# Attention's value products with the values on the left, the probabilities of two query heads moving, and the result turned back

## What is computed

```python
def sink_attention(q, k, v, mask, sink):
    s = jnp.einsum('bnqhgd,bnchd->bnhgqc', q, k).astype(jnp.float32) * (HEAD_DIM ** -0.5)
    s = jnp.where(mask[None, :, None, None], s, NEG_BIG)
    sink_col = jnp.broadcast_to(sink..., s.shape[:-1] + (1,))
    prob = jax.nn.softmax(jnp.concatenate([s, sink_col], axis=-1), axis=-1)[..., :-1]
    return jnp.einsum('bnhgqc,bnchd->bnqhgd', prob.astype(v.dtype), v)

def window_attention_prompt(q, k, v, sink):
    # blocks of WINDOW = 128 queries; each reads the 16 meta rows, the block before and itself
    keys = jnp.concatenate([meta(k), band(kb)], axis=2)
    vals = jnp.concatenate([meta(v), band(vb)], axis=2)
    ...

def merge(att_o, ga, hg_o, gh, hg_norm_w, w_out):
    att = att_o.reshape(*lead, ATT_WIDTH) * jax.nn.silu(ga)
    ...
```

## Time and profile before

| | before |
|---|---|
| median of 3 runs | 1170.9 us (1170.76 to 1171.3) |
| the profiled execution | 1167.6 us |
| its span | 1165.8 us |
| TensorE busy | 1129.7 us, 97% of the span |
| VectorE, ScalarE, GpSimd busy | 61%, 37%, 31% |
| mean granted clock of TensorE | 0.992 |

### The profile page before, as it was taken

One profiled execution on the slowest core, in us unless ns is written; L12 is line 12 of the kernel. 1 busy time (PEld: TensorE's weight loads), 2 busy tenths in 40 slices (PEclk: granted clock), 3 DMA queues, 4 the chain that ended last, 5 costly groups with the idle time before them and its releaser, 6 DMA issues.

```text
span 1165.8 us, 26052 instructions
## 1 busy us (share of the span) xinstructions
PE 1129.7 (97%) x9506; PEld 943.5 (81%) x9506; DVE 712.0 (61%) x1847; ACT 430.4 (37%) x1242; POOL 362.4 (31%) x420
## 2 busy tenths in 40 slices
PE   6999999999999999998879999999999999999998
PEld 5877888888888888887667888888888888688887
DVE  6657666666666666668745556555665666655443
ACT  6412212222222222215124555555565665433230
POOL 0003333333333333334422223222322227243331
PEclk9999999999999999999989999999999999999999
DMA  8532111111111111127022511211121133443431
GB/s 281 182 109 74 50 62 63 63 63 63 63 63 54 63 63 63 46 82 270 26 91 74 201 46 45 81 54 45 46 79 59 46 106 133 158 146 144 150 139 72
DMA packets 49391, 108.33 MB, mean 93 GB/s; under 512 B 5088, under 2 KB 17888, under 8 KB 49312
## 3 DMA queue, kind: packets, MB, share of 16 engines
q1 hardware_dynamic: 49328, 107.51, 25.9%
HBM read 70.23 MB, written 38.26 MB: 93 GB/s over the span
## 4 chain that ended last, share of the span: by engine, by line
PE 88%; DVE 5%; POOL 3%; issue 1%; ACT 1%; DMA 1%; SPq 1%; DVEq 0%; POOLq 0%; ACTq 0%
PE h_bank_b L917 5%; PE h_bank_a L917 5%; PE h_bank_b L919 5%; PE h_bank_b L918 5%; PE h_bank_a L919 5%; PE h_bank_a L918 5%; PE o_bank L2621 4%; PE o_bank L2623 4%; PE o_bank L2622 4%; PE h_bank_t L901 3%; PE a_bank_a L1891 3%; PE a_bank_a L1892 3%; PE a_bank_a L1893 3%; PE a_bank_b L1891 3%; PE a_bank_b L1892 3%; PE a_bank_b L1893 3%
## 5 line engine op out<-in xcount | busy, mean ns | idle before, releaser
L917 PE MATMUL h_bank_b<-h_w_hi,h_h_hi 128*128 128x512 f32 x256 | 106.5, 416 | 0.1
L1682 DVE CUSTOM_DVE_ANT_0 a_sm<-a_sc,a_hidden,a_neg_sink 128x272 f32<-128x272 f32 x128 | 59.0, 499 | 74.1 <-PE a_sc L1921 74.0
L917 PE MATMUL h_bank_a<-h_w_hi,h_h_hi 128*128 128x512 f32 x256 | 103.1, 403 | 0.0
L919 PE MATMUL h_bank_b<-h_w_hi,h_h_lo 128*128 128x512 f32 x256 | 100.9, 394 | 0.0
L918 PE MATMUL h_bank_b<-h_w_lo,h_h_hi 128*128 128x512 f32 x256 | 100.4, 392 | 0.0
L919 PE MATMUL h_bank_a<-h_w_hi,h_h_lo 128*128 128x512 f32 x256 | 99.9, 390 | 0.0
L918 PE MATMUL h_bank_a<-h_w_lo,h_h_hi 128*128 128x512 f32 x256 | 99.8, 390 | 0.0
L1488 ACT ACTIVATE a_prb<-a_sm,a_neg_m 128x256 f32<-128x256 f32 x128 | 64.2, 502 | 70.9 <-DVE a_neg_m L1682 70.8
L1891 PE MATMUL a_bank_a<-a_w_hi,a_h_hi 128*128 128x512 f32 (+1 forms) x208 | 77.0, 370 | 6.1 <-DMA a_h_lo<-h_split 6.1
L1892 PE MATMUL a_bank_a<-a_w_lo,a_h_hi 128*128 128x512 f32 (+1 forms) x208 | 74.1, 356 | 0.0
L1893 PE MATMUL a_bank_a<-a_w_hi,a_h_lo 128*128 128x512 f32 (+1 forms) x208 | 74.1, 356 | 0.0
(11 more groups left out here) (327 smaller groups left out, 3121.3 us busy)
## 6 DMA issues: line engine op xcount, KB each, us to landing
h_split<-h_h_hi SPq DMA_DIRECT2D x17, 512.0 KB, 3.0
h_split<-h_h_lo SPq DMA_DIRECT2D x17, 512.0 KB, 3.9
a_h_hi<-h_split SPq DMA_DIRECT2D x17, 512.0 KB, 3.4
a_h_lo<-h_split SPq DMA_DIRECT2D x17, 512.0 KB, 4.3
h_x<-x_prompt SPq DMA_DIRECT2D x16, 512.0 KB, 3.4
o_m<-mixed SPq DMA_DIRECT2D x16, 512.0 KB, 4.0
o_x<-x_prompt SPq DMA_DIRECT2D x16, 512.0 KB, 4.3
y_prompt<-o_x SPq DMA_DIRECT2D x16, 512.0 KB, 2.6
```

What stands on the lines that cost most here:

```text
L917: pe.matmul(out[:, :], h_hi[t.slot][:, k, :], hi, start=(k == 0), stop=False)
L919: ins = pe.matmul(out[:, :], h_lo[t.slot][:, k, :], hi, start=False, stop=(k == KT - 1))
L1682: ins = dve.tensor_tensor_reduce(SM[j % 2][:, i, :], sc[:, i, 0:KEYS], hidden[:, mask, :], -SCALE, neg_sink[:, h:h + 1], ALU.add, ALU.min, ...
```

## The change

The roles in the value products are exchanged: the 64 columns of a value head are the left operand, and the turned probabilities of two query heads of its group, 256 columns, are the moving one. The two value heads write the lower and the upper 64 partitions of `bank_o`, that is, stand at the left and the right half of the array. To make this possible a pair now holds one query head of each group (`head(j, i)`), PTS is twice as large and laid out by value head and block of keys, and there are two values steps for a tile, each for two pairs. VMD, the block-diagonal matrix of the meta values, is laid out in four blocks of 128 columns, and its product is four products with PMT moving. The result stands with the channels on the partitions; it is copied out by ScalarE (`copy_o`, to MIX), turned back by four transposes (`turn_o`) into `bank_o`, and normalized from there to MIX, which `mix` then multiplies in place (o_nat is gone).

The order changes with it. On VectorE `o_norm(last)` moves behind `maxima(t0, 0)`. On ScalarE `copy_o(last)` stands between `gate(t0)` and `place_q(t0, 1)`. On TensorE `turn_o(last)` stands behind `scores(t0, 0)`, and the query projection is split four and four instead of five and three. GpSimd's order stays. At the stage's end some pieces of the output stage's list are cut finer, so that `copy_o` and `turn_o` of the last tile fit between them.

```diff
+        PTS = sb("pts", [P, KVH, 2, 2, P])
...
+        def head(j, kv):
+            return kv * G_HEADS + j
...
-                sp.dma_start(VMD[h * META:(h + 1) * META, h * HD:(h + 1) * HD], V_meta[:, kv * HD:(kv + 1) * HD]).then_inc(v_meta_spread, 16)
+                kv, g = h // G_HEADS, h % G_HEADS
+                at = g * P + kv * HD
+                sp.dma_start(VMD[h * META:(h + 1) * META, at:at + HD], V_meta[:, kv * HD:(kv + 1) * HD]).then_inc(v_meta_spread, 16)
...
-                wait(pool, mix_stored, 16 * t.n)
-                pool.tensor_tensor(MIX[:, :], o_nat[:, :], G[t.slot][:, :], ALU.mult).then_inc(mix_done, 1)
+                pool.tensor_tensor(MIX[:, :], MIX[:, :], G[t.slot][:, :], ALU.mult).then_inc(mix_done, 1)
...
+            def copy_o(t):
+
+                act.wait_ge(o_ready, 2 * t.n - 1)
+                wait(act, mix_stored, 16 * t.n)
+                act.activation(MIX[:, :], bank_o[:, :], ACT.Copy).then_inc(o_copied, 1)
...
                 gate_plus(t0)
+                place_v(t0)
+                maxima(t0, 0, mask)
                 if tail:
                     o_norm(last)
-                place_v(t0)
-                maxima(t0, 0, mask)
...
-                for i in range(2):
-                    h = 2 * j + i
-                    kv = h // (AH // KVH)
-                    c, out = slice(kv * HD, (kv + 1) * HD), bank_o[:, h * HD:(h + 1) * HD]
-
-                    pe.matmul(out, PTS[:, i, 0:P], V[0][:, c], start=(h == 0), stop=False)
-                    ins = pe.matmul(out, PTS[:, i, P:2 * P], V[1][:, c], start=False, stop=False)
+                for block in range(2):
+                    for kv in range(KVH):
+                        c = slice(kv * HD, (kv + 1) * HD)
+                        ins = pe.matmul(bank_o[c, 2 * a * P:2 * (a + 1) * P], V[block][:, c],
+                                        PTS[:, kv, block, :, :].rearrange("p g q -> p (g q)"),
+                                        start=(a == 0 and block == 0), stop=False, skip_group_check=True)
                 ins.then_inc(pv_done, 1)
-                if j == 3:
-                    pe.matmul(bank_o[:, :], PMT[:, :], VMD[:, :], start=False, stop=True).then_inc(o_ready, 1)
+                if a == 1:
+                    for g in range(G_HEADS):
+                        c = slice(g * P, (g + 1) * P)
+                        ins = pe.matmul(bank_o[:, c], VMD[:, c], PMT[:, :], start=False, stop=True, skip_group_check=True)
+                    ins.then_inc(o_ready, 1)
+
+            def turn_o(t):
+
+                pe.wait_ge(o_copied, t.n)
+                for g in range(G_HEADS):
+                    c = slice(g * P, (g + 1) * P)
+                    ins = pe.transpose(bank_o[:, c], MIX[:, c], ident[:, :])
+                ins.then_inc(o_ready, 1)
```

More of the change, by code:

```diff
@@ L1542, in iteration @@
                 gate(t0)
+                if tail:
+                    copy_o(last)
                 place_q(t0, 1)
@@ L1580, in scalar @@
             gate(t0)
+            copy_o(tile(0, TILES - 3))
             place_q(t0, 1)
@@ L1610, in scalar @@
             place_p(end, 3)
+            yield
+            copy_o(end)
             yield
@@ L1709, in place_v @@
                 dve.wait_ge(v_copied, t.n + 1)
-                wait(dve, pv_done, 4 * (t.n - 1))
+                wait(dve, pv_done, 2 * (t.n - 1))
                 if first_tile(t):
@@ L1841, in vector @@
             gate_plus(t0)
-            o_norm(last)
             place_v(t0)
             maxima(t0, 0, t0.slot)
+            o_norm(last)
             k_stats(end)
@@ L2036, in tensor @@
             project(t2, kv_bank(t2), 2, range(4, 8)).then_inc(g_proj, 1)
-            values(t1, 2)
             turn_p(t1, 3)
+            pe.wait_ge(v_meta_spread, AH * 16)
             pe.wait_ge(k_placed, 3)
@@ L2047, in iteration @@
                 if tail:
-                    values(last, 3)
+                    values(last, 1)
                 pe.wait_ge(q_placed, 2 * t0.n - 1)
@@ L2054, in iteration @@
                 pe.wait_ge(g_copied, t0.n + 1)
-                project(t1, q_bank(t1), 1, range(0, 5))
+                if tail:
+                    turn_o(last)
+                project(t1, q_bank(t1), 1, range(0, 4))
                 turn_p(t0, 0)
                 scores(t0, 1)
-                project(t1, q_bank(t1), 1, range(5, 8)).then_inc(q_proj, 1)
-                values(t0, 0)
+                project(t1, q_bank(t1), 1, range(4, 8)).then_inc(q_proj, 1)
                 turn_p(t0, 1)
@@ L2064, in iteration @@
                 project(t1, kv_bank(t1), 2, range(0, 4))
-                values(t0, 1)
+                values(t0, 0)
                 turn_p(t0, 2)
@@ L2070, in iteration @@
                 project(t1, kv_bank(t1), 2, range(4, 8)).then_inc(g_proj, 1)
-                values(t0, 2)
                 turn_p(t0, 3)
@@ L2084, in tensor @@
             project(end, kv_bank(end), 0, range(0, 4))
-            values(tile(0, TILES - 3), 3)
+            values(tile(0, TILES - 3), 1)
             pe.wait_ge(q_placed, 2 * t0.n - 1)
@@ L2090, in tensor @@
             pe.wait_ge(g_copied, t0.n + 1)
+            turn_o(tile(0, TILES - 3))
             project(end, q_bank(end), 1, range(0, 4))
@@ L2114, in tensor @@
             yield
-            values(t0, 3)
+            values(t0, 1)
             pe.wait_ge(q_placed, 2 * end.n - 1)
@@ L2123, in tensor @@
             scores(end, 2)
-            values(end, 0)
             turn_p(end, 1)
@@ L2127, in tensor @@
             scores(end, 3)
-            values(end, 1)
+            values(end, 0)
             turn_p(end, 2)
             yield
-            values(end, 2)
             turn_p(end, 3)
             yield
-            values(end, 3)
+            values(end, 1)
+            yield
+            turn_o(end)
             yield
@@ L2826, in _ @@
             next(o)
+            next(a)
+            next(o)
         @block.vector
```

57 lines of the change are left out of this document (29 added, 28 removed).

## The result

The changed kernel takes **1194.1 us** (median of 5 runs, 1191.4 to 1196.1) against 1170.8 us before (median of 5, 1169.9 to 1171.3): ratio 1.0209, 95% interval 1.0195 to 1.0224. It is **23.4 us slower**. The forecast was 1191.3 us.

What follows compares the result with a forecast made beforehand. TensorE, busy 307.27 of 307.30 us, was taken to bound the attention stage, two feeders only just in time; +20.5 us for 13 iterations and -0.1 at the ends gave 20.4, so 1191.3 us, range 1175 to 1213.

Steps and rivals of the forecast that it cites:

- TensorE's own work: Values steps, meta product and turning back on TensorE: 3.88 us a tile instead of 4.23, a gain of 0.35 us.
- The two halves at once: In a values step, products at the array's left and right half run together: four rounds of 0.22, 1.28 us a step.
- the halves take turns: Rival: the array's halves run one after the other, values step 1.94 us or more, total 1212 to 1225; chance 0.10.
- Steps 1 to 6 of the chain: Pair 0's maxima, normalization, gate product, keys' power, keys' split, pair 1's exponentials; TensorE waits 1.3 us, turn 0.85 later.
- Step 4: Keys' power on GpSimd, 0.69 us: input ready at S+2.6, queues behind the product with the gate, ends S+4.31.
- The wait for the low halves: TensorE, before turning the next tile's queries, waits for their low halves from GpSimd: a new wait of 0.69 us.
- The iteration: One loop iteration of the attention stage, 13 alike (tiles 2 to 14): +1.58 us each, +20.5 us together.
- Tile 1: Tile 1's wait for pair 2's exponentials shrinks and the slow clock there goes: -1.9 us.
- Tile 15: Tile 15 has the two new waits but loses small ones at the hand-over: +0.8 us.
- The hand-over: Tile 16, into the output stage: copy, turning back and later gate product lengthen the chain TensorE waits for: +1.0 us.
- The clock in the loop: Forecast: clock stays 1.00. Rival: each iteration's waits drop it to half level, total 1205 to 1213; chance 0.08.
- TensorE's list decides: Rival: waits don't grow, so the 0.35 us a tile and tile 1's 1.9 are gained, total 1164; chance 0.08.

Runs made afterwards that it cites:

- one_half: Changed kernel with all four value products of a step writing the low 64 partitions, so part of the result is left out: 1218.8 us (one run).
- first_head_only: Changed kernel with the second value head's products left out, four instructions a values step instead of eight: 1195.0 us (one run).
- mix_behind: Changed kernel with GpSimd's product with the gate of the last tile moved behind the keys' power: 1190.7 us.
- turn_early: Changed kernel with tile 15's result turned back ahead of the output products between tile 16's scores and the rest, not behind them: 1190.4 us.
- all_loads: As all_moves, with SyncE issuing the output stage's first loads ahead of the store of tile 14's result: 1172.7 us (10 runs).
- before_norm_moved: Kernel before the change, value products untouched, with only the normalization moved behind the maxima of pair 0 (and the same in tile 15): 1182.2 us.
- all_moves: Changed kernel with normalization and gate product behind the keys, first values step behind pair 3's scores, tile 15's result turned back ahead of output products: 1178.2 us.

## Why the prediction was right, and where its sizes were off

The forecast was 1191.3 us, in a range of 1175 to 1213; it is 1194.1. Step by step:

- **TensorE's own work**, a gain of 0.35 us a tile: measured about 0.5. Two terms were off, against each other. A values step was put at 1.28, with four rounds of 0.22 and the last way out inside; it measures 1.01, and 1.15 with 0.09 on the product ahead and 0.05 on the turn behind. The meta product was put at 0.88 and measures 1.00: its first instruction costs 0.1 more than the others. The turning back costs the forecast 0.44 (770.33 to 770.69, and 0.08 on the product behind). Together 2 x 1.15 + 1.00 + 0.44 = 3.74 us against 4.23. The iteration says the same: 24.93 us less some 1.97 of waits (on average 1.09 ahead of pair 1, 0.78 ahead of the queries, 0.10 ahead of pair 0) is 22.96, before 23.63 less 0.17 is 23.46. TensorE's busy time falls by less, from 23.63 to 23.33 (287.61/307.30 of 24.93), because the last product ahead of a wait counts as busy to its end, some 0.15 us beyond its share.
- **The two halves at once**: taken over from 32-column products. Right, and shown by one_half and first_head_only. The rival "the halves take turns" gave 1212 to 1225, and the kernel that enforces it took 1218.8.
- **Steps 1 to 6 of the chain** between scores and turned pair 1: forecast S+8.30, measured S+8.20. Maxima end at S+1.43 as forecast, normalization at S+2.11 (2.12), the product with the gate at S+3.48 (3.58), the keys' power at S+4.29 (4.31), the maxima of pair 1 start at S+5.51 (5.6). The numbers are right, but the reason was half of the truth. Step 4 says that the power's input is ready at S+2.6 and queues on GpSimd. The input came at S+3.51, since VectorE itself was held by the product; so undoing the queue alone (mix_behind) gave back 0.43 us an iteration (318.44 us for the 13), 3.4 us in all, where the queue theory expected 12.
- **The wait for the low halves**, forecast 0.69, measured 0.78 (788.15 to 788.93, the turned meta probabilities being worth 0.11). Right, in all 12 iterations of the window.
- **The iteration**: forecast +1.58, measured +1.30, 16.8 us instead of 20.5. The miss is mainly the values step, 0.13 cheaper twice, and the chain, 0.1 earlier; the meta product, 0.12 dearer, went the other way. (The tile shown here, 7, is one of the longer ones: +1.40.)
- **Tile 1**, forecast -1.9: this gain did not come. From the scores of pair 0 to those of tile 2 it is 33.70 us, before 30.31 (the +4.6 and -1.2 of the table). But in that stretch the clock stood at its half level for 10.2 us in this execution and for 3.4 in before's; turn_early's execution, with the same list there and also 3.4 us of it, takes 30.72. The granted clock from 594 to 634 us was 0.74, 0.83 and 0.87 in the three. So 3.0 of the 27.9 us between the two profiled executions are no effect of the change, and the tile costs 0.4 us more instead of 1.9 less. I counted on the slow clock going away, and a stretch of it stayed in every profiled run; and I left out of tile 1 the wait for the low halves, which stands there too:

```profile
PE a_bank_t L1929 <- POOL a_qs L1395: 1.0, 1, 1.0
```

- **Tile 15**, forecast +0.8, measured +1.3. 0.6 of it is the wait for the sample rows, which I had not seen.
- **The hand-over**, forecast +1.0: this is the term that was furthest off, it measures +4.2, and 1.9 more behind it, where the clock stood at its half level for 6.8 us. I counted the last tile's own chain (copy, turning back, later product) and not who queues behind tile 15's product with the gate: GpSimd's 16 sums. turn_early shows 2.2 us of it directly; that the 2.0 left go back to the same product is argued from its lag, not tested.
- **The clock in the loop**: no fall in it, mean 1.00 with waits of 1.0 and 0.6 us. The rival fell. At the hand-over, with 4.97 us of waiting, it did fall.
- **A small slip in the sum**: the break-even for the rival "TensorE's list decides" (added waits below 0.26 us) left out the 0.11 us that TensorE waits for pair 0 in step 6; with them it is the 0.35 of own work. Nothing hung on it.

The change thus costs in the profile 16.8 us in the loop, 1.3 at tile 15, 6.1 at and behind the hand-over and some 0.6 in tile 1 and ahead of it: 24.8, and 3.0 more for the clock of that execution. The median's +23.4 (22.8 to 26.2 by its interval) fits that. The mechanism in the loop was forecast, and the total's closeness is in part luck: the loop was 3.7 us too much, the ends, put at -0.1, were 8 us too little.

What stays open: all_loads is 1.8 us slower than before. Its 13 iterations cost 1.0 us more, in which the two small waits for the exponentials (4.5 us in 12 iterations) are paid for in part by TensorE's smaller own work, and its stretch from tile 16's scores to the first turned block 2.0 us more (32.80 against 30.76). Whether a version with both removed would be faster than the kernel before wasn't tried.

## What to carry to other kernels

Where TensorE is full, a change that gives it 0.5 us less work an iteration is decided by the slack of its feeders, and that stands in the timeline: 0 and 0.18 us here, so 16 us of the loss were order. When a step is moved on one engine, follow it through every queue that takes its result, the DMA queue and the next stage's work behind it included: the late product with the gate had three customers (the keys' power, the sums of the next stage, the load behind the store). Each cost some us: 8.6 in before_norm_moved's loop for the first, 2 to 4 at the hand-over for the second, 5.6 from all_moves to all_loads for the third. And compare stretches between two profiles from a point behind the last clock fall, not whole spans.

## What the runs showed of the hardware

- Products with 64 left columns at partitions 0 and 64 run at the same time: 1.01 us for eight instructions of 256 columns in two halves, 1.87 us (1.94 with the way out) in one, 1.00 us for four in one. In the two orders tried the pairing didn't depend on the list, four and four did as well as by turns (1.02).
- Some instructions of VectorE that start while GpSimd multiplies two SBUF tiles don't end before it, however small they are: a TENSOR_SCALAR of 128x2 took 1.17 and 1.25 us instead of 0.17, a CAST of 128x256 0.86 instead of 0.29, an addition of two SBUF tiles of 128x8 (`a_den`) 0.68 to 0.78 instead of 0.15. The maxima's operation (0.50) and the SCALAR_TENSOR_TENSOR (0.48 for two), which read a product bank, were as fast as alone.
- Between executions of one and the same list the half-clock stretch in tile 1 lasted 3.4 us (turn_early) or 10.2 (the changed kernel), worth 3.0 us of the time.
